# Eight modulation chunks for one condition: sums over channel tiles on VectorE, partition sums on TensorE

## The reference, cut to what matters

```python
for i in range(DEPTH_2):                       # 2 layers
    sh1, sc1, g1, sh2, sc2, g2 = jnp.split((silu_c @ mod_w[i] + mod_b[i])[:, None, :], 6, axis=-1)
    a_lat = modulate(rms_norm(h_lat, norm_mix_g[i]), sh1, sc1)
    csh1, csc1, cg1, csh2, csc2, cg2 = jnp.split(silu_cctx @ mod_w[i] + mod_b[i], 6, axis=-1)
    a_ctx = modulate(rms_norm(h_ctx, norm_mix_g[i]), csh1, csc1)
    ...
    h_lat = h_lat + g1 * o_lat
    h_lat = h_lat + g2 * swiglu(modulate(rms_norm(h_lat, norm_ffn_g[i]), sh2, sc2), ...)
    if not last:
        h_ctx = h_ctx + cg1 * o_ctx
        h_ctx = h_ctx + cg2 * swiglu(...)
```

## Time and profile before

| | |
|---|---|
| time, median of 3 runs (lowest to highest) | 1395.94 us (1393.19 to 1397.42) |
| span of the profiled execution | 1400.9 us |
| TensorE busy in it | 1325.8 us (95%) |
| VectorE busy | 833.3 us (59%) |
| ScalarE busy | 549.3 us (39%) |
| GpSimd busy | 25.3 us (2%) |
| transferred from HBM | 216.74 MB |
| chain that ended last: TensorE, VectorE, ScalarE | 78%, 11%, 5% |

### The profile page before, as it was taken

One profiled execution on the slowest core, in us unless ns is written; L12 is line 12 of the kernel. 1 busy time (PEld: TensorE's weight loads), 2 busy tenths in 40 slices (PEclk: granted clock), 3 DMA queues, 4 the chain that ended last, 5 costly groups with the idle time before them and its releaser, 6 DMA issues.

```text
span 1400.9 us, 16622 instructions
## 1 busy us (share of the span) xinstructions
PE 1325.8 (95%) x6816; PEld 1062.1 (76%) x6816; DVE 833.3 (59%) x1148; ACT 549.3 (39%) x733; POOL 25.3 (2%) x60
## 2 busy tenths in 40 slices
PE   6999879999999999999999999999989989799998
PEld 5877758888787787867777777787866666688887
DVE  5665666658664554663434344445776777667777
ACT  5354354455331222432121313123465664455542
POOL 0000000000000000000000000000021110000000
PEclk9999889999999999999999999999999999899999
DMA  8436374544555423346353544412122231345441
GB/s 328 184 120 255 120 285 180 186 175 181 190 201 209 167 109 116 120 188 232 121 218 143 198 163 182 178 42 83 46 85 82 76 121 61 120 167 195 180 180 60
DMA packets 23928, 218.79 MB, mean 156 GB/s; under 512 B 3121, under 2 KB 8241, under 8 KB 10673
## 3 DMA queue, kind: packets, MB, share of 16 engines
q1 hardware_dynamic: 21472, 209.67, 40.3%
q10 hardware_dynamic: 1520, 4.98, 0.9%
q0 software_dynamic: 864, 3.15, 0.7%
HBM read 216.74 MB, written 1.05 MB: 155 GB/s over the span
## 4 chain that ended last, share of the span: by engine, by line
PE 78%; DVE 11%; ACT 5%; issue 3%; DMA 2%; POOL 0%; SPq 0%; DVEq 0%; ACTq 0%
PE bank L540 19%; PE bank L541 18%; PE bank L542 18%; PE bank L552 9%; PE bank L553 5%; DVE w_lo L1621 4%; PE mod_ps L589 3%; PE turned L568 2%; ACT w_hi L1119 2%; PE bank L962 2%; DVE scaled L1662 2%; DVE gated L1976 1%; DMA raw<-in_w_branch 1%; DMA raw<-in_w_out 1%; PE small L608 1%
## 5 line engine op out<-in xcount | busy, mean ns | idle before, releaser
L1621 DVE TENSOR_TENSOR w_lo<-raw,w_hi 128x2048 fp32r<-128x2048 f32 (+4 forms) x168 | 338.4, 2054 | 83.9 <-ACT w_hi L1119 83.7
L1119 ACT ACTIVATE w_hi<-raw 128x2048 fp32r<-128x2048 f32 (+4 forms) x168 | 280.3, 1716 | 206.8 <-PE bank L542 180.6
L540 PE MATMUL bank<-act_parts,w_hi 128*128 128x512 f32 (+1 forms) x600 | 225.1, 375 | 1.8 <-DVE act_parts L1646 1.8
L552 PE MATMUL bank<-act_parts,w_hi 128*128 128x512 f32 x608 | 218.1, 403 | 6.4 <-DVE act_parts L1646 4.2
L541 PE MATMUL bank<-act_parts,w_hi 128*128 128x512 f32 (+1 forms) x600 | 221.8, 370 | 0.0
L542 PE MATMUL bank<-act_parts,w_lo 128*128 128x512 f32 (+1 forms) x600 | 221.6, 369 | 0.0
L553 PE MATMUL bank<-act_parts,w_lo 128*128 128x256 f32 x608 | 171.8, 283 | 0.0
L540 PE MATMUL bank<-w_hi,h_hi 128*128 128x512 f32 x392 | 155.8, 398 | 6.9 <-DVE h_lo L1898 3.5
L542 PE MATMUL bank<-w_hi,h_lo 128*128 128x512 f32 x392 | 154.1, 393 | 0.0
L541 PE MATMUL bank<-w_lo,h_hi 128*128 128x512 f32 x392 | 154.0, 393 | 0.0
L552 PEld LDWEIGHTS bank<-act_parts,w_hi 128*128 128x128 f32 x608 | 115.6, 190 | 36.2 <-DVE act_parts L1646 4.6
(11 more groups left out here) (261 smaller groups left out, 1652.2 us busy)
## 6 DMA issues: line engine op xcount, KB each, us to landing
raw<-in_ffn SPq DMA_DIRECT2D x35, 2048.0 KB, 7.7
raw<-in_mlp SPq DMA_DIRECT2D x24, 2048.0 KB, 7.7
raw<-in_mod_gate SPq DMA_DIRECT2D x7, 2048.0 KB, 7.7
raw<-in_conv_in SPq DMA_DIRECT2D x8, 1536.0 KB, 7.1
raw<-in_w_gates SPq DMA_DIRECT2D x4, 2048.0 KB, 8.2
raw<-in_w_branch SPq DMA_DIRECT2D x4, 2048.0 KB, 7.9
raw<-in_mla_q SPq DMA_DIRECT2D x4, 1152.0 KB, 5.1
raw<-in_w_out SPq DMA_DIRECT2D x2, 2048.0 KB, 8.2
```

Source lines behind the costliest of these rows:

```text
L540: te.matmul(dst, sh, mh, start=(j == 0), stop=False)
L552: te.matmul(b[:, :].rearrange("p (a t) -> p a t", a=2), sh, act_parts[:, :, 0, j, :], start=(j == 0), stop=False)
L1119: act.activation(w_hi[:, s, part], raw[:, at % 2, part], ACT.Copy).then_inc(hi_ready, 1)
L1621: ve.tensor_tensor(w_lo[:, s, part], raw[:, at % 2, part], w_hi[:, s, part].bitcast(f32), ALU.subtract).then_inc(lo_ready, 1)
```

## The change

The eight chunks get a kind of their own in the stream (`SUMMED`); their places in it stay. TensorE no longer multiplies them. VectorE multiplies channel tile k of the chunk (128 x 512) by the condition's column k and adds it to a running sum, eight instructions a chunk (`mod_sums`): four at a time around each pair of results of an up window, or one behind each result of a down window. What is left is a sum over the 128 partitions: for shifts and scales four products of a 128 x 128 block of the sum with one column of ones (`column_sums`), for gates one product of a 128 x 128 block of ones with the sum (`gate_sum`). The slot of such a chunk is free when its eighth VectorE instruction has ended.

```diff
@@ slot_free (sync)
-                if STREAM[at - 2][3]:
+                if STREAM[at - 2][3] == PRODUCT:
                     sp.wait_ge(mod_done, MOD_AT.index(at - 2) + 1)
+                elif STREAM[at - 2][3] == SUMMED:
+                    sp.wait_ge(mod_summed, KT * (SUM_AT.index(at - 2) + 1))
                 else:
                     sp.wait_ge(lo_ready, 2 * (WEIGHT_AT.index(at - 2) + 1))
@@ gpsimd
+            pool.wait_ge(x_ready, 10)
+            gate_bias(2, (0,))
             pool.wait_ge(x_ready, 12)
-            gate_bias(2, (0,))
             gate_bias(3, (1,))
@@ tensor
+            def column_sums(i):
+                te.wait_ge(ones_ready, 1)
+                te.wait_ge(mod_summed, KT * (i + 1))
+                small_bank()
+                for b in range(4):
+                    last = te.matmul(small[:, b:b + 1], part_sum[:, i % 3, b * P:(b + 1) * P], all_ones[:, 0:1], start=True, stop=True)
+                last.then_inc(small_done, 1)
+            def gate_sum(i, dst, src):
+                te.wait_ge(mod_summed, KT * (4 + i + 1))
...
+                te.matmul(dst[:, :], all_ones[:, :], src, start=True, stop=True).then_inc(gate_sum_done, 1)
@@ norm_both (tensor)
                 if first:
                     mod_product(0, 2)
+                else:
+                    gate_sum(0, small, part_sum[:, 1, :])
+                    gate_sum(1, mod_ps, part_sum[:, 2, :])
@@ the twelve windows (tensor)
             for i in range(4):
-                mod_product((3 * i) % 4 if i < 3 else 1, 4 if i < 3 else 2)
+                if i < 2:
+                    mod_product(3 * i, 4)
                 gate_up()
                 if i == 1:
                     mod_turn()
-                mod_product((3 * i + 1) % 4 if i < 3 else 0, 4 if i < 3 else 2)
+                if i == 0:
+                    mod_product(1, 4)
+                if i == 2:
+                    column_sums(1)
                 gate_up()
+                if i == 0:
+                    mod_product(2, 4)
                 if i == 2:
-                    mod_turn()
-                mod_product((3 * i + 2) % 4 if i < 2 else 0 if i == 2 else 1, 4 if i < 2 else 2)
+                    column_sums(2)
                 down0_all()
+                if i in (1, 2):
+                    column_sums(0 if i == 1 else 3)
@@ the latents (tensor)
-            gate_rows(7, 0, 0)
...
-            gate_rows(7, 1, 0)
...
-            gate_rows(8, 0, 0)
+            gate_sum(2, small, late_sum[0][:, :])
...
-            gate_rows(8, 1, 0)
+            gate_sum(3, mod_ps, late_sum[1][:, :])
@@ vector
+            def mod_sums(i, kts):
+                at = SUM_AT[i]
+                dst = part_sum[:, i % 3, :] if i < 6 else late_sum[i - 6][:, :]
+                for k in kts:
+                    src, by = raw[:, at % 2, k * COLS:(k + 1) * COLS], cond[:, k, 6:7]
+                    if k == 0:
+                        ve.wait_ge(loaded[at % 2], 16 * (at // 2 + 1))
+                        ve.tensor_scalar(dst, src, by, None, ALU.mult).then_inc(mod_summed, 1)
+                    else:
+                        ve.wait_ge(mod_summed, KT * i + k)
+                        ve.scalar_tensor_tensor(dst, src, by, dst, ALU.mult, ALU.add).then_inc(mod_summed, 1)
@@ hidden_chunk (vector)
                 split(width)
+                if columns is not None:
+                    column_read(columns)
                 for f in range(2):
+                    if sums is not None:
+                        mod_sums(sums, range(4 * f, 4 * f + 4))
@@ down_gated (vector)
                 split()
+                if columns is not None:
+                    column_read(columns)
                 for cb in range(2):
                     for tt in range(2 * NT):
                         add_gated(tt, cb, tt // NT, False)
+                        if sums is not None:
+                            mod_sums(sums, range(2 * NT * cb + tt, 2 * NT * cb + tt + 1))
```

More of the change, by code:

```diff
@@ L57, with summed @@
 )
+WEIGHT, PRODUCT, SUMMED = range(3)
 def _stream():
     def weight(section, i, width=CHUNK):
-        return (section, i, width, False)
+        return (section, i, width, WEIGHT)
     def mod(section, i):
-        return (section, i, CHUNK, True)
+        return (section, i, CHUNK, PRODUCT)
+    def summed(section, i):
+        return (section, i, CHUNK, SUMMED)
     out = [weight("w_in", 0), weight("w_in", 1), weight("w_kv", 0, 2048)] + [weight("w_gates", i) for i in range(4)]
@@ L78, in _stream @@
     out += [weight("ffn0_first", 0), mod("mod_gate1", 0), weight("ffn0_half", 0, 2048), mod("mod_gate1", 1)]
-    second = [mod("mlp", 13), mod("mlp", 15), mod("mlp", 19), mod("mlp", 21)] + [mod("ffn0", 4 * i + 1) for i in range(4)]
-    second += [mod("mod_gate2", 0), mod("mod_gate2", 1), mod("mod_gate3", 0), mod("mod_gate3_half", 0)]
+    second = [mod("mlp", 13), mod("mlp", 15), mod("mlp", 19), mod("mlp", 21)] + [summed("ffn0", 4 * i + 1) for i in range(4)]
+    second += [summed("mod_gate2", 0), summed("mod_gate2", 1), summed("mod_gate3", 0), summed("mod_gate3_half", 0)]
     for i in range(4):
@@ L92 @@
 STREAM = _stream()
-WEIGHT_AT = [i for i, c in enumerate(STREAM) if not c[3]]
-MOD_AT = [i for i, c in enumerate(STREAM) if c[3]]
+WEIGHT_AT = [i for i, c in enumerate(STREAM) if c[3] == WEIGHT]
+MOD_AT = [i for i, c in enumerate(STREAM) if c[3] == PRODUCT]
+SUM_AT = [i for i, c in enumerate(STREAM) if c[3] == SUMMED]
 WEIGHTS = len(WEIGHT_AT)
@@ L311, in build @@
     mod_done = S("mod_done")
+    mod_summed = S("mod_summed")
+    ones_ready = S("ones_ready")
+    gate_sum_done = S("gate_sum_done")
+    gate_sum_read = S("gate_sum_read")
+    late_gate_bias_loaded = [S("gate2_bias_loaded"), S("gate3_bias_loaded")]
     mod_row_ready = S("mod_row_ready")
@@ L428, in gate_bias @@
                 for k in slots:
-                    pool.dma_start(gate[:, k, :], src).then_inc(gate_bias_loaded, 16)
+                    landed = gate_bias_loaded if g < 2 else late_gate_bias_loaded[g - 2]
+                    pool.dma_start(gate[:, k, :], src).then_inc(landed, 16)
             pool.wait_ge(gemm_done, UNITS_BEFORE_CONV)
@@ L1091, in _ @@
             down1(1, 2, 0)
-            assert n.n["chunk"] == WEIGHTS and n.n["mod"] == len(MOD_AT) and n.n["batch"] == 8
+            assert n.n["chunk"] == WEIGHTS and n.n["mod"] == len(MOD_AT) and n.n["batch"] == 5
         @block.scalar
@@ L1691, in modulated, with coefs, column_read, gate_sum_added @@
                          act_dst(act_hi, q, half, t), act_dst(act_lo, q, half, t)) for half in range(2)]
-            def coefs(c, name, layer, scale_at):
-                chained(ve.scalar_tensor_tensor(coef[:, c, :, :], mod_col[:, scale_at:scale_at + KT, :], 1.0,
-                                                gain_cols(name, layer * KT, KT).to_broadcast([P, KT, 2]), ALU.add, ALU.mult))
+            def coefs(c, name, layer, scale_at, conds=2):
+                chained(ve.scalar_tensor_tensor(coef[:, c, :, 0:conds], mod_col[:, scale_at:scale_at + KT, 0:conds], 1.0,
+                                                gain_cols(name, layer * KT, KT).to_broadcast([P, KT, conds]), ALU.add, ALU.mult))
+            def mod_sums(i, kts):
[6 more added lines that the diff above has]
+                        ve.tensor_scalar(dst, src, by, None, ALU.mult).then_inc(mod_summed, 1)
+                    else:
+                        ve.wait_ge(mod_summed, KT * i + k)
+                        ve.scalar_tensor_tensor(dst, src, by, dst, ALU.mult, ALU.add).then_inc(mod_summed, 1)
+            def column_read(i):
+                n.step("small")
+                ve.wait_ge(small_done, n.step("mod_small"))
+                at = 48 + 4 * i
+                ve.tensor_tensor(mod_col[:, at:at + 4, 0], small[:, 0:4], col("mod_b", at, 4), ALU.add).then_inc(small_read, 1)
+            def gate_sum_added(i, src):
+                ve.wait_ge(late_gate_bias_loaded[i // 2], 16)
+                ve.wait_ge(gate_sum_done, i + 1)
+                dst = gate[:, i // 2, (i % 2) * COLS:(i % 2 + 1) * COLS]
+                ve.tensor_tensor(dst, src[:, :], dst, ALU.add).then_inc(gate_sum_read, 1)
             def mod_read(batch):
@@ L2014, in _, with hidden_chunk @@
             norm_both(lambda tt: add_gated(tt, 1, tt // NT, True), 1, 0, "norm_ffn", 16, False)
-            def hidden_chunk(first, width=CHUNK, gates=False):
+            def hidden_chunk(first, width=CHUNK, gates=False, sums=None, columns=None):
                 split(width)
+                if columns is not None:
+                    column_read(columns)
                 for f in range(2):
+                    if sums is not None:
+                        mod_sums(sums, range(4 * f, 4 * f + 4))
                     if gates:
@@ L2035, in down_gated @@
                         add_gated(tt, cb, tt // NT, False)
+                        if sums is not None:
+                            mod_sums(sums, range(2 * NT * cb + tt, 2 * NT * cb + tt + 1))
```

(18 more changed lines are left out.)

26 lines of the change are left out of this document (14 added, 12 removed).

## The result

The changed kernel takes **1435.1 us** (median of 4 runs, 1429.7 to 1435.9) against 1396.7 us (4 runs, 1393.2 to 1400.7) for the kernel before beside it: ratio 1.026, 95% interval 1.0239 to 1.028. It is 38.4 us slower; the forecast was +38.0 us, to 1434.

What follows compares the result with a forecast made beforehand. SyncE's queue, standing at full slots, was taken as the bound: −14.8 − 0.9 + 3.6 + 49.0 of stalls − 1.3 + 2.4 of clock gave +38.0 us, 1434 us, with 1412 to 1452 us holding some 8 times in 10.

Steps and rivals of the forecast that it cites:

- The queue decides: SyncE's queue stands at a full slot, 146 us for TensorE's product; what empties the slot sets when the next transfers start.
- The times of the releases: In the eight windows, a chunk's eighth sum frees its slot late; modulation and weight transfers then go out together.
- lone transfer: On SyncE's queue, a 2 MB transfer by itself was taken to land after 7.8 us.
- The stalls: TensorE's waits for VectorE in windows 2 to 8, walked window by window: 49.0 us in all.
- the low clock: TensorE's granted clock falls after stalls of 3 to 9 us: +2.4 us, with 0 and +12 as ends.
- that is swallowed: Low-clock cost, 1.5 us of products per 3 us at half clock, vanishes in windows where TensorE waits for VectorE afterwards.
- Products gone and column sums come: On TensorE, eight products go, −14.8 us, and one `mod_turn`, −0.9; four `column_sums` come at 0.9 each, +3.6.
- The 1.3 us for the gate rows: Four TensorE gate rows become same-size products, two moving into idle time ahead of the latents: −0.9 to −1.7, taken −1.3.
- A: Rival: transfers come in time and the gain stays, −13.4 us, 1382.5 us; needs window 2's weights 9.7 us behind issue; 8%.
- B: Rival: feedback there but weaker, 1401 to 1412 us; each 1 us less of landing takes about 7 off; 10%.
- C: Rival: VectorE and the clock make it worse, from 14.5 us to landing on, +50 and more, 1448 to 1462 us; 8%.
- The rule beside A: Optimize the highest-occupancy engine first, here TensorE at 95% busy; by it the time would fall to A's.

Runs made afterwards that it cites:

- weights-first kernel: Changed kernel with SyncE issuing the weight transfer behind each of the eight summed chunks ahead of it: 1382.5 us, ratio 0.9879 to the kernel before.
- single sum: Changed kernel with seven of each chunk's eight VectorE sums left out, the last keeping its place and freeing the slot: 1407.3 us, ratio 1.0067 to the kernel before.
- half transfer: Changed kernel with only the first half (1 MB of 2) of each of the eight summed chunks transferred: 1411.6 us, ratio 1.0094 to the kernel before.
- sums ahead everywhere: Changed kernel with all eight sums of a chunk ahead of VectorE's weight split in up and down windows: 1390.2 us, ratio 0.9942 to the kernel before.

## Why the prediction was right, step by step

**The queue decides** (the row on which the forecast rested). Shown by the weights-first kernel from one side and by the single sum from the other. The mechanism was forecast as well as the number.

**The times of the releases.** In the trace of the changed kernel the first window starts at 723.95 us, which is taken as t = 0 here. The pairs were forecast at t = 16.0, 51.7, 79.0, 106.3, 142.2, 169.6, 196.7 and 232.4 (the last three are not written out there; they follow from windows 6 to 8 repeating 3 to 5), that is 740.0, 775.7, 803.0, 830.3, 866.2, 893.6, 920.7 and 956.4 us; SyncE issued the first of each pair at 740.2, 775.3, 802.7, 829.4, 866.4, 894.3, 921.1 and 956.1. None is off by 1 us. The terms of the walk, from the changed kernel's rows, 720 to 960 us:

```profile
L1752 DVE SCALAR_TENSOR_TENSOR part_sum<-raw,cond,part_sum 128x512 f32<-128x512 f32 x42 | 31.5, 749 | 0.8
L1749 DVE TENSOR_SCALAR part_sum<-raw,cond 128x512 f32<-128x512 f32 x6 | 2.9, 478 | 0.0
```

A sum takes 0.75 us as taken from the earlier trace rows; the first of a chunk 0.48 us, not 0.55. The column sums of one chunk (start us, us), 0.95 us where 0.9 was taken between the bounds of nothing and 1.85:

```profile
795.61 0.95 PE L635 MATMUL small<-all_ones,part_sum 128*128 128x1 f32 x8
```

The second of a pair landed 12.1 to 13.3 us after its own issue, 12.4 to 13.7 behind the first's (12.9 taken). The "lone transfer" of 7.8 us was misread: the earlier trace rows show a pair, and 7.8 is its first. A transfer by itself took 7.6 to 8.5 us in the weights-first kernel, so the number did no harm.

**The stalls were too large on paper, the low clock too small.** Each wait of TensorE over 1 us, against the forecast:

| window | forecast us | measured us |
|---|---|---|
| 2 (down) | 3.2 | 3.09 |
| 3 (up) | 4.1 | 1.81 |
| 4 (up) | 5.9 and 3.0 | 3.62 |
| 5 (down) | 9.2 | 7.78 |
| 6 (up) | 5.0 | 3.05 |
| 7 (up) | 6.6 and 3.0 | 4.53 and 1.34 |
| 8 (down) | 9.0 | 8.73 |
| sum | 49.0 | 34.0, with the small ones 35.0 |

The first stall is right to 0.1 us. Those behind it are smaller because TensorE came to them late: it had worked at the low clock. While VectorE's side sets when TensorE may go on, it makes no difference to the end whether TensorE idles until then or works slowly. This isn't so everywhere: from 850.3 to 864.2 us, the first part of it at 0.50, the chain runs through TensorE's products, and VectorE waits for them twice, 0.19 and 0.64 us; behind the last stall (from 941.0 us) the low clock is paid in full, too. Two terms were mis-sized, the stalls' (49.0 us) and the clock's (+2.4 us with 0 to +12 as ends). In the 4 us stretches of the eight windows in which the clock was below 0.95, busy time times what was missing of the clock comes to about 14 us (the 4.00 us at 0.50 from 852 us count 2.0). The 34.9 us that TensorE was idle and the 14 us of low clock are 49, where I had 51.4. Both terms were off by 12 to 14 us, in opposite directions, and I had named the reason ("that is swallowed") but took it off the clock's term instead of the stalls'. The sum was right since it had been walked from release to release; by the terms it was partly luck.

**The stage and the rest.** Products gone and column sums come, with the measured 3.8: −14.8 − 0.9 + 3.8 = −11.9. With the 49, +37. The stage, by the last `silu` of the network (it starts at 952.55 us before and at 992.08 after, less the 0.95 us by which the windows began later), grew by 38.6 us; 1.5 us of it are not accounted for. Behind it the two traces come 6.5 us closer, to spans of 1433.9 and 1400.9. The forecast had said that nothing would change there by more than 2 us. No run shows that the change did it, and most of it is in the clock: the profiled run of the kernel before has more low clock behind the network (the earlier trace rows show that near 973 us, and it was 0.50 and 0.67 in two stretches of 4 us from 1048 us on) than the run of after. Busy time times what was missing of the clock comes to 10.6 us in the one and 5.7 in the other. The profiled run of before was also one of the slower of its kernel. The medians differ by 38.4. The 1.3 us for the gate rows cannot be told apart from that and stay unproven.

**The rivals.** A (gain stays, 1382.5 us) was the right price for another queue: "if the queue served the weights first, A would hold", and with the weights first the kernel takes 1382.5 us. That the two agree to the tenth is luck, since by differences it is −13.4 against −15.4 us. A's own condition was wrong. It made window 2 decide, with a landing 9.7 us behind the pair's issue. In the half transfer five of seven pairs landed after 9.7 to 9.9 us and window 2 had no wait over 0.3 us, yet later windows stalled (the first at the end of window 4, 2.6 us) and the kernel was 13.6 us slower than the kernel before. B's slope of 7 us per microsecond of landing was nearly borne out by the half transfer, at about 8.5. C's condition, a landing of 14.5 us or more, didn't come up. The rule beside A, from the Trainium skill, Perfetto Trace Analysis, section Identifying the Most-Contended Engine, to optimize the engine of highest occupancy first, pointed the wrong way here: the change took work off the busiest engine, gave VectorE the release of a slot, and cost 38.4 us. The Trainium skill adds in that section that TensorE's headroom is not to be judged by its matmul busy time but, among others, by the share of its weight loads; by that share, 76% in the earlier trace rows, it is still the busiest. The Trainium skill, Perfetto Trace Analysis, section Optimization Strategy, says to find the gaps on that engine and make what blocks them start sooner or end faster; that is what the weights-first kernel does to the changed one, and the trace agrees (waits 35.0 to 0.6 us).

## What to carry to other kernels

Moving work to an engine with free time also moves the release of whatever buffer that work reads. Look up which queue waits for the release, and what independent transfer stands behind it: issue that one first. If a late release feeds back into the next (late landing, late split, late release), walk the loop window by window, and count TensorE's slow clock inside the stalls where another engine sets the pace, beside them where TensorE does.

## What the runs showed of the hardware

**A stall costs more than itself, unless a loop pays for both.** TensorE's idle time from 720 to 960 us (240 us less its busy time) against what the kernel takes more than the weights-first one (each by its difference to the kernel before beside it):

| kernel | idle us | more than weights-first, us |
|---|---|---|
| changed | 34.9 | 53.8 |
| half transfer | 17.2 | 29.0 |
| only the last sum | 19.0 | 24.3 |
| sums ahead everywhere | 5.5 | 7.2 |
| weights first | 2.2 | 0 |

Of the weights-first kernel's 2.2 us, 1.7 lie behind the network. In the other four the last column exceeds the idle time by 19, 12, 5 and 2 us. TensorE's busy time at a lowered clock in this stretch, times what was missing of the clock, is 13.9, 11.1, 5.0 and 1.6 us in the same order, and nothing with the weights first. So the low clock accounts for the excess to within 1 us in three kernels; in the changed one 5 us stay open. Two long stalls (last sum only, 9.1 and 8.7 us) cost less of it than about as many microseconds in six shorter ones (half transfer, 0.8 to 5.2 us).

**A pair of transfers.** Of the changed kernel, the first pair:

```profile
raw<-in_ffn SPq DMA_DIRECT2D x2, 2048.0 KB, 10.3
```

The two landed after 8.0 and 12.6 us, while the weights-first kernel's six in a row from 735 to 800 us, mostly apart, had a median of 8.1:

```profile
raw<-in_ffn SPq DMA_DIRECT2D x6, 2048.0 KB, 8.1
```

The first of a pair is hardly slowed, and the second pays: it lands 5.0 us behind the first, 2.1 MB in that time. The half transfer ahead of it saves 3.1 us of the second's landing (12.6 to 9.5).
